# A hybrid decoder step on Trainium2: o's norm from four column groups spread by a transfer, and stacked rows of v and k made by VectorE and DRAM instead of TensorE

## What is computed

```python
xn = rms_norm(x, g_pre)
u_a, v_a, z_a, q_b, k_b, v_b, z_b, a_lr, m_a, m_b = split_cols(xn @ w_in)
v_a = rms_norm(v_a, g_v)
y_a = chunk_spatial_gate(u_a, v_a, w_s, b_s) * silu(z_a)
log_a = log_sigmoid(a_lr @ w_a2 + b_a) / GATE_TAU
# gated linear attention: 4 heads, dk 128, dv 256, evaluated in blocks
#   o = (masked q~ k~^T) v + q~ S ;  S = exp(b_last) * S + k_d^T v
o, s_new = gla(q * DK**-0.5, k, v, log_a, s0)
y_b = rms_norm(o, g_o).reshape(B, L, E_B) * silu(z_b)      # norm over the 256 of each head
m = sigmoid(m_a) * (y_a @ w_pa) + sigmoid(m_b) * (y_b @ w_pb)
h = x + rms_norm(m @ w_o, g_post)
h = h + sigmoid(h @ w_pg) * (p @ w_pe)
```

## Time and profile before

| | us |
|---|---|
| three runs, median (lowest to highest) | 966.81 (965.63 to 966.93) |
| the profiled execution | 965.56 |
| its span | 963.8 |
| TensorE busy | 957.8 |
| VectorE busy | 554.8 |
| ScalarE busy | 401.0 |
| GpSimd busy | 107.9 |

### The profile page before, as it was taken

How to read it: one execution, slowest core, us unless ns; L and a number is a source line. 1 busy time by engine, 2 the same in 40 slices (tenths; PEclk the granted TensorE clock), 3 DMA queues, 4 the chain that set the end, 5 groups by cost and what they waited for, 6 DMA issues and landing times.

```text
span 963.8 us, 17471 instructions
## 1 busy us (share of the span) xinstructions
PE 957.8 (99%) x6696; PEld 946.4 (98%) x6696; DVE 554.8 (58%) x751; ACT 401.0 (42%) x497; POOL 107.9 (11%) x103
## 2 busy tenths in 40 slices
PE   9999999999999999999999999999999999999998
PEld 7999999999999999999999999999999999999998
DVE  7858658536787687544444544444455444696443
ACT  7445344432253434443434344343433333464331
POOL 1000001011124542000000000000002333100000
PEclk9999999999999999999999999999999999999999
DMA  9535435475745345444444444544447444346541
GB/s 354 193 111 174 152 112 153 147 246 192 246 155 163 122 141 157 150 139 166 151 147 144 147 151 134 170 149 143 147 149 275 152 149 147 119 136 213 178 153 41
DMA packets 52966, 155.83 MB, mean 162 GB/s; under 512 B 6208, under 2 KB 17344, under 8 KB 52928
## 3 DMA queue, kind: packets, MB, share of 16 engines
q1 hardware_dynamic: 39456, 139.77, 43.5%
q10 hardware_dynamic: 13472, 15.53, 4.8%
HBM read 147.68 MB, written 7.60 MB: 161 GB/s over the span
## 4 chain that ended last, share of the span: by engine, by line
PE 99%; DMA 1%; ACT 0%; DVE 0%; SPq 0%; issue 0%; DVEq 0%; ACTq 0%
PE bank L1152 29%; PE bank L1153 29%; PE bank L1154 29%; PE bank L1440 1%; PE bank L1437 1%; PE bank L1434 1%; PE bank L1206 1%; PE bank L1215 1%; PE bank L1209 1%; DMA x_sb<-in_x_t 1%; PE bank L1180 0%; PE bank L1178 0%; PE bank L1179 0%; PE bank L1325 0%; PE bank L1380 0%; PE bank L1300 0%
## 5 line engine op out<-in xcount | busy, mean ns | idle before, releaser
L642 DVE TENSOR_TENSOR w_lo<-w_raw,w_hi 128x1024 fp32r<-128x1024 f32 x252 | 316.4, 1261 | 346.6 <-ACT w_hi L343 179.0
L1152 PE MATMUL bank<-x_hi,w_hi 128*128 128x320 f32 x1216 | 378.4, 311 | 0.0
L1154 PE MATMUL bank<-x_hi,w_lo 128*128 128x320 f32 x1216 | 376.2, 309 | 0.0
L1153 PE MATMUL bank<-x_lo,w_hi 128*128 128x320 f32 x1216 | 376.2, 309 | 0.0
L343 ACT ACTIVATE w_hi<-w_raw 128x1024 fp32r<-128x1024 f32 x148 | 155.7, 1058 | 262.1 <-PE bank L1154 241.0
L1152 PEld LDWEIGHTS bank<-x_hi,w_hi 128*128 128x128 f32 x1216 | 228.4, 188 | 2.2 <-issue 1.8
L1153 PEld LDWEIGHTS bank<-x_lo,w_hi 128*128 128x128 f32 x1216 | 228.4, 188 | 0.2
L1154 PEld LDWEIGHTS bank<-x_hi,w_lo 128*128 128x128 f32 x1216 | 228.4, 188 | 0.0
L547 ACT ACTIVATE w_hi<-w_raw 128x1024 fp32r<-128x1024 f32 x96 | 101.7, 1059 | 104.9 <-PE bank L1154 104.8
L1152 PE MATMUL bank<-m_hi,w_hi 128*128 128x320 f32 x448 | 138.6, 309 | 0.0
L1153 PE MATMUL bank<-m_lo,w_hi 128*128 128x320 f32 x448 | 138.6, 309 | 0.0
(11 more groups left out here) (232 smaller groups left out, 931.1 us busy)
## 6 DMA issues: line engine op xcount, KB each, us to landing
w_raw<-in_w_units SPq DMA_DIRECT2D x259, 512.0 KB, 3.3
state_dec<-in_s ACTq DMA_DIRECT2D x8, 512.0 KB, 5.8
out_st_dec<-state_dec ACTq DMA_DIRECT2D x8, 512.0 KB, 4.7
h<-in_x_t ACTq DMA_DIRECT2D x4, 640.0 KB, 6.9
out_y<-pe_out ACTq DMA_DIRECT2D x16, 160.0 KB, 2.2
x_sb<-in_x_t SPq DMA_DIRECT2D x7, 320.0 KB, 8.6
w_raw<-in_w_units ACTq DMA_DIRECT2D x2, 256.0 KB, 3.8
out_st_prompt<-state ACTq DMA_DIRECT2D x1, 512.0 KB, 2.9
```

What stands on the lines that cost most here:

```text
L642: dve.tensor_tensor(wlo[:, q], raw[:, q], whi[:, q].bitcast(F32), ALU.subtract).then_inc(lo_ready, 1)
L1152: pe.matmul(acc, h, hi[:, k0 + k, :], start=first and k == 0, stop=False)
L1153: pe.matmul(acc, h, lo[:, k0 + k, :], start=False, stop=False)
L1154: m = pe.matmul(acc, l, hi[:, k0 + k, :], start=False, stop=last and k == UK - 1)
```

## The change

For o's norm, the four sums go to four groups of 32 output rows of bank 4 instead of to four banks. One scaling, one reciprocal and one root then serve all heads (`r_heads`, step z_a 5). One row of each group is stored to DRAM (`r_rows`), and in the next step a transfer reads the four rows back to all 128 partitions (`r_o`). GpSimd waits for that transfer.

For the stacked rows, VectorE transposes the new positions first, those of v at t = 0 and 1 and those of k (new, 8 transposes of 32x128) at t = 1. At t = 2 ScalarE rounds both and VectorE forms the remainders (`v_parts`, `k_parts`, 64 partitions). ScalarE's queue stores the rounded parts at t = 3 and the remainders at t = 4, each twice, and at t = 5, after all eight stores, loads `vx_t` and `kx_t` from DRAM in eight transfers, one for each head and tensor. TensorE's 24 transposes and ScalarE's six bank copies are gone; the first `sequences` waits for the loads.

```diff
-        v_x = at("v_stacked", M0 + 4 * slot, [P, DEC_B, DV // P, HB, 4, DEC_L])
-        k_x = at("k_stacked", M0 + slot, [P, DEC_B, HB, 4, DEC_L])
+        v_parts = at("v_parts", M0 + 4 * slot, [DEC, 2, EB], F32R)
+        k_parts = at("k_parts", M0 + slot, [DEC, 2, HB * DK], F32R)
+        k_ts = at("k_tokens_dec", M0 + 3 * slot, [DEC, HB * DK])
         o_sb = at("o", M0 + 2 * slot, [P, KE, T])
...
         r_o = at("r_o", M0 + 6 * slot, [P, HB, T])
+        r_heads = at("r_heads", M0 + 5 * slot, [P, T])
...
         VAT_STEPS = (0, 0, 0, 0, 4, 4, 4, 4, 0, 3, 5, 5, 3)
-        O_NORM = tuple(S_ZA + 5 + 2 * h for h in range(HB))
+        O_NORM = S_ZA + 5
         D64, D128, DDEC = NBLK, NBLK + 4, NBLK + 5
...
         r_ready = sem("r_ready")
+        r_stored, r_spread = sem("r_heads_stored"), sem("r_o_loaded")
         logits_done = sem("logits_done")
...
         vt_ready = sem("vt_ready")
-        x_hi_parts, x_lo_parts = sem("stacked_rounded"), sem("stacked_split")
-        xt_done, xt_copied = sem("stacked_transposed"), sem("stacked_copied")
+        kts_ready = sem("kts_ready")
+        parts_hi, parts_lo = sem("parts_rounded"), sem("parts_split")
+        rows_stored, rows_loaded = sem("rows_stored"), sem("rows_loaded")
         ps_done, ps_copied = sem("prompt_state_done"), sem("prompt_state_copied")
...
+        r_rows = nc.dram_tensor("r_rows", (HB, T), F32, kind="Internal").ap()
+        v_rows = nc.dram_tensor("v_rows", (DEC_B, 2, 2, DEC_L, EB), F32, kind="Internal").ap()
+        k_rows = nc.dram_tensor("k_rows", (DEC_B, 2, 2, DEC_L, HB * DK), F32, kind="Internal").ap()
         block = ctx.enter_context(nc.Block())
...
-                    for n in (0, 2):
-                        for i in range(2):
-                            act.activation(v_x[:, :, i, :, n, :].bitcast(F32R), new_tokens(v_sb[:, i::2, :]), ACT.Copy)\
-                               .then_inc(x_hi_parts, 1)
-                    for n in (0, 1):
-                        act.activation(k_x[:, :, :, n, :].bitcast(F32R), new_tokens(k_dec), ACT.Copy)\
-                           .then_inc(x_hi_parts, 1)
                     act.wait_ge(kdt_done, 1)
                     copy_banks(kd_t[:].rearrange("p c n -> p (c n)"), (4, 5), P, kdt_copied)
+                if t == 2:
+                    act.wait_ge(vt_ready, 2 * (P // BLK))
+                    act.activation(v_parts[:, 0, :], v_ts[:], ACT.Copy).then_inc(parts_hi, 1)
+                    act.wait_ge(kts_ready, 2 * (P // BLK))
+                    act.activation(k_parts[:, 0, :], k_ts[:], ACT.Copy).then_inc(parts_hi, 1)
+                if t in (3, 4):
+                    part = t - 3
+                    if part:
+                        act.wait_ge(parts_lo, 2)
+                    else:
+                        act.wait_ge(parts_hi, 2)
+                    for twin in range(2):
+                        act.dma_start(v_rows[:, twin, part], v_parts[:, part, :].bitcast(F32)).then_inc(rows_stored, 16)
+                        act.dma_start(k_rows[:, part, twin], k_parts[:, part, :].bitcast(F32)).then_inc(rows_stored, 16)
                 if t == 5:
-                    act.wait_ge(xt_done, 1)
-                    copy_banks(vx_t[:].rearrange("p b n -> p (b n)"), (4, 5, 6, 7), P, xt_copied)
+                    act.wait_ge(rows_stored, 16 * 8)
+                    for h in range(HB):
+                        rows = slice(BLK * h, BLK * h + BLK)
+                        act.dma_start(vx_t[rows, :, :].bitcast(F32), v_rows[:, :, :, :, DV * h:DV * h + DV]
+                                      .rearrange("b m n t v -> (m n t) b v")).then_inc(rows_loaded, 16)
+                        act.dma_start(kx_t[rows, :, :].bitcast(F32), k_rows[:, :, :, :, DK * h:DK * h + DK]
+                                      .rearrange("b m n t v -> (m n t) b v")).then_inc(rows_loaded, 16)
                 if t == 6:
-                    act.wait_ge(xt_done, 2)
-                    copy_banks(kx_t[:].rearrange("p b n -> p (b n)"), (2, 3), P, xt_copied)
                     act.wait_ge(ps_done, 1)
...
                         load_s0(b)
-            def root_o(h):
-                root(3 + h, r_o[:, h, :], r_o[:, h, :])
...
                     act.dma_start(O["cv"].rearrange("i p t -> p i t"), cv[:]).then_inc(cv_stored, 16)
-                if s in O_NORM:
-                    root_o(O_NORM.index(s))
+                if s == O_NORM:
+                    root(3, r_heads[:, :], r_heads[:, :])
+                    act.wait_ge(r_ready, 3)
+                    act.dma_start(r_rows, r_heads[0:P:BLK, :]).then_inc(r_stored, 16)
+                if s == O_NORM + 1:
+                    act.wait_ge(r_stored, 16)
+                    act.wait_ge(s0_stored[5], 16)
+                    act.dma_start(r_o[:].rearrange("p h t -> p (h t)"), r_rows.rearrange("h t -> (h t)").unsqueeze(0)
+                                  .to_broadcast([P, HB * T])).then_inc(r_spread, 16)
...
                 act.activation(yhi[1][:, j, :], o_sb[:, j, :], ACT.Copy, scale=col(C_GO, j)).then_inc(y_rounded, 1)
-                if s in O_NORM:
-                    root_o(O_NORM.index(s))
...
+            def k_to_tokens(n):
+                ct, pf = n // 4, n % 4
+                rows, to = slice(BLK * ct, BLK * ct + BLK), slice(BLK * pf, BLK * pf + BLK)
+                dve.transpose(k_ts[rows, :].rearrange("p (h f) -> p h f", f=DK)[:, :, to],
+                              k_dec[to, :, SEQ + BLK * ct:SEQ + BLK * ct + BLK]).then_inc(kts_ready, 1)
             def v_to_tokens(n):
-                ct, pf = n // 4, n % 4
+                ct, pf = (n // 4 + SEQ // BLK) % (T // BLK), n % 4
                 dst = v_t[:, ct // 4, :] if ct < SEQ // BLK else v_ts
...
                 if t == 1:
-                    dve.wait_ge(x_hi_parts, 6)
-                    for n in (1, 3):
-                        for i in range(2):
-                            dve.tensor_tensor(v_x[:, :, i, :, n, :].bitcast(F32R), new_tokens(v_sb[:, i::2, :]),
-                                              v_x[:, :, i, :, 0, :], ALU.subtract).then_inc(x_lo_parts, 1)
-                    for n in (2, 3):
-                        dve.tensor_tensor(k_x[:, :, :, n, :].bitcast(F32R), new_tokens(k_dec), k_x[:, :, :, 0, :],
-                                          ALU.subtract).then_inc(x_lo_parts, 1)
+                    for n in range(2 * (P // BLK)):
+                        k_to_tokens(n)
+                if t == 2:
+                    for n, (parts, x) in enumerate(((v_parts, v_ts), (k_parts, k_ts))):
+                        dve.wait_ge(parts_hi, n + 1)
+                        dve.tensor_tensor(parts[:, 1, :], x[:], parts[:, 0, :].bitcast(F32), ALU.subtract)\
+                           .then_inc(parts_lo, 1)
                 if t == 0:
...
                     v_to_tokens(n)
-            def variance_o(h):
-                dve.wait_ge(s0_stored[5], 16)
-                dve.wait_ge(sum_done, 3)
-                variance(r_o[:, h, :], bank[4 + h][:, 0:T], DV)
...
                 gate_input(s, KE + b)
-                if s in O_NORM:
-                    variance_o(O_NORM.index(s))
+                if s == O_NORM:
+                    dve.wait_ge(sum_done, 3)
+                    variance(r_heads[:, :], bank[4][:, 0:T], DV)
                 if b == 1:
...
                 split_lo(s)
-                if s in O_NORM:
-                    variance_o(O_NORM.index(s))
                 sums(s)
...
             for j in range(KE):
-                pool.wait_ge(r_ready, 3 + j // 2)
+                pool.wait_ge(r_spread, 16)
                 then(pool.tensor_tensor(o_sb[:, j, :], o_sb[:, j, :], r_o[:, j // 2, :], ALU.mult))
...
-            def stack_rows(x, banks):
-                for c in range(4 * len(banks)):
-                    m = pe.transpose(bank[banks[c // 4]][:, P * (c % 4):P * (c % 4) + P], x[:, P * c:P * c + P], ident)
-                m.then_inc(xt_done, 1)
             def o_prompt(n):
...
                     m.then_inc(kdt_done, 1)
-                if t == 5:
-                    pe.wait_ge(x_lo_parts, 6)
+                if t == 6:
                     pe.wait_ge(kdt_copied, 2)
                     pe.wait_ge(att_copied, 7)
-                    stack_rows(v_x[:].rearrange("p b i h n t -> p (b i h n t)"), (4, 5, 6, 7))
-                    stack_rows(k_x[:].rearrange("p b h n t -> p (b h n t)"), (2, 3))
-                if t == 6:
-                    pe.wait_ge(xt_copied, 4)
                     pe.wait_ge(vt_ready, 4 * T // BLK)
...
                 if c == 1:
-                    pe.wait_ge(xt_copied, 6)
+                    pe.wait_ge(rows_loaded, 16 * 2 * HB)
                     pe.wait_ge(ps_copied, 2)
...
                     for h in range(HB):
-                        m = sum_partitions(bank[4 + h][:, 0:T], o_sum[:, h, :])
+                        m = pe.matmul(bank[4][BLK * h:BLK * h + BLK, 0:T], ones[:, 0:BLK], o_sum[:, h, :], start=True,
```

(7 more changed lines are left out.)

## The result

| | before | changed |
|---|---|---|
| runs, median (lowest to highest), us | 966.16 (965.38 to 966.93), 5 runs | 970.11 (968.99 to 972.29), 5 runs |
| ratio to before | | 1.0043, 95% interval 1.0032 to 1.0053 |
| the profiled execution, its span | 965.56, 963.8 | 972.29, 970.6 |

The change made the kernel 4.0 us slower. 3.0 faster was forecast (966.8 to 963.8), with a range up to 966.3. A second measurement of the same kernel on another occasion gave 969.61 against 965.8. The profiled execution is the slowest of the five, so what it adds up to lies above the 4.0 of the medians.

A forecast was written before the change was run, and what follows sets the result against it. TensorE was taken as the bound, busy 957.8 of 963.8 us. Terms -2.62 - 1.5 + 1.1 = -3.0 took the median from 966.8 to 963.8 us; the range ran from 962.7 less 0.5 to 966.3.

The forecast's parts named there:

- TensorE's savings: 24 transposes gone at z_b step 5, -2.62 us; o's four sums of squares in one grouped round of 0.65, -1.5 us.
- the 0.14 read off the a_lr product: Most that both edges of the grouped form could cost: four a_lr rounds exceed four single sums by 0.14 us.
- VectorE's delay and the wait of 1.1: Ahead of the prompt state, z_b step 6: VectorE's v transposes come late and TensorE waits, +1.1 us.
- ScalarE's queue: Store issues in z_b steps 3 and 4 take 2.1 us a group, hidden behind VectorE with 0.65 to spare: no cost.
- signs that it named for being wrong: No idle or over 2 us before the prompt state; ScalarE's roundings held; TensorE waiting for a transfer; new u-step waits.
- The rival that named this mechanism: The stores hold ScalarE: issues of 0.8 us make the wait 1.8, of 1.2 make it 5; typical -1.0, chance 0.14.
- Cases that lose time: Slower outcomes: late rows and the far end of the stores' case, chance 0.07 together.
- The transfers: Eight row loads take 5 to 17 us, start by 177 and are first used at 209: hidden.
- The norm's round trip: o's norm through DRAM, between root and GpSimd's first use: 18.6 of 20.1 us available, so zero cost.

The follow-up runs named there:

- experiment 7: Changed kernel with the stores on SyncE's queue and the prompt state moved to the end of z_b step 7: 961.66 us against 965.8 before.
- experiment 3: Changed kernel with the eight stores issued from SyncE's queue and not ScalarE's: 963.81 us against 965.82 before.
- experiment 9: Changed kernel with the eight stores dealt out two a step over z_b steps 3 to 6, loads in step 7: 963.42 us against 965.99 before.
- experiment 8: Changed kernel with the DRAM rows laid out position first, a store being 64 rows and not 8 by 8: 966.55 us against 965.8 before.
- experiment 5: The changed kernel measured again, unchanged, against the kernel before: 969.61 us against 965.8.

## Why the prediction was wrong

- **TensorE's savings: right.** 2.62 gone, and the sums 0.68, the upper end, where 0.65 was taken. The drain that the Trainium skill warns of (TensorEngine Tiling, "Key Properties") cost no more than the 0.14 read off the a_lr product (0.68 less the 0.54 of one sum). The whole 4.1 is measured in experiment 7.
- **VectorE's delay and the wait of 1.1: right as a mechanism,** and right in size where ScalarE is on time: 1.22 in experiments 3 and 9.
- **ScalarE's queue: the step that failed.** "An issue blocks the sequencer for 0.4, and for 0.55 in a row of several [...] So the stores are hidden behind VectorE with 0.65 us to spare, twice." The groups measured 4.7 and 4.8 us and not 2.1 (4.1 to 4.5 in four other profiles with the same stores). The spare time was 0.5 and not 0.65, since VectorE waits for the first of the two roundings behind a group and not only for the second. So each group held `tmp` up by 2.2 to 2.4 us, 4.6 in all at step 5, and TensorE's wait became 5.3. The `tmp` of step 4, which the prediction had in time, held TensorE by another 0.4. Two of the signs that it named for being wrong came: a wait of over 2 us, and ScalarE's roundings of steps 4 and 5 held by its queue. The price came from loads of another shape, issued three in a row; nothing in the trace of before had four stores in a row, and the term had no upper bound in the sum, only in a rival. What makes the third or fourth store of a group long stays open: by experiments 8 and 9 it takes the stores ahead of it, and their shape has a part in it.
- **The price of waiting: left out.** A wait was costed at its length. With a wait of 5.3 us the granted clock was at half for the job behind it, and that job took 3.2 us more, 0.24 of it the restart (1.9 more after a wait of 4.6 in experiment 5). The rival that named this mechanism ("at 1.2 each it is 5 us and the gain is gone") met the issue's mean (1.2) and the wait (5.3), yet not the clock, and its typical result was set at -1.0 with a chance of 0.14. Cases that lose time held 0.07 in all.
- **The transfers: right in what mattered.** The last load was issued at 185.6 and none took over 12.7 us to land, so all were there 20 us ahead of their use at 218.7. **The norm's round trip: right.** The root's four rows went out at 319.8, `r_o` was issued at 325.2 and landed 7.1 later, at 332.3; GpSimd took it at 336.7, behind its own z_a work.

## What to carry to other kernels

When work leaves a busy TensorE for other engines, first write down which wait of TensorE ends next and how many us are in hand there; removing 2.6 us from TensorE also takes 2.6 us from the cover of everything behind it. Count an engine's DMA issues as work of that engine, priced for the whole group that stands together: deal them out, or give them to a queue whose engine has nothing else to do. And price a wait of TensorE with what the clock takes from the job that follows it: here 1.9 and 3.2 us on top of waits of 4.6 and 5.3, and 0.24 on top of 1.2.

## What was not expected of the hardware

- Issue time on a queue is not a constant. Loads of the old states took 0.38 and 0.53 us; stores of 256 KB and 128 KB with an 8 by 8 DRAM side took 0.57 to 1.17 while two stood together. Of four in a row the longest took 1.6 to 2.6 on ScalarE's queue and 1.4 to 2.8 on SyncE's, and a group 4.1 to 4.8 and 3.4 to 4.6 in all. With the DRAM side as 64 rows a group took 3.0 to 3.4.
- TensorE's clock fell to half in the profiled executions with 4.6 us of idle time and more ahead of the prompt state, and not in those with 1.2 and 2.5; useless matmuls in the same stretch kept it full.
- TensorE's first weight products took 1.27 to 1.41 us for each of the first groups of four in four of the twelve profiled executions, and 0.75 to 0.83 in the other eight. By the first attention products the first kind is 1.2 us later on average, which hides most of a gain of 1.5 in a single profile.
